# Two hybrid layers, two mixture-of-experts layers: the last experts are taken out of the loop and the overflow section moves ahead of the row selections

## The reference, cut to what matters

```python
def _hier_moe(h, w_group, b_group, w_router, b_router, w_gate, w_up, w_down):
    ...                       # each token: one of 4 groups, then the best 2 of its 8 experts
    def expert_block(args):
        xe, e = args
        return (jax.nn.silu(xe @ w_gate[e]) * (xe @ w_up[e])) @ w_down[e]
    ...                       # y of a token: its two experts' rows, weighted and summed

for i in range(DEPTH):        # DEPTH = 2; 512 tokens, and 256 context tokens in layer 0
    ...
    y = _hier_moe(tokens, ...)
    x = x + gt_f * y[:b * n].reshape(b, n, d)
    if not last:
        xc = xc + gtc_f * y[b * n:].reshape(xc.shape)
return _rmsnorm(x, g_final)
```

## Time and profile before

| | us |
|---|---|
| median of 3 runs | 2984.36 |
| lowest, highest run | 2981.99, 2987.34 |
| time of the profiled execution | 2984.36 |
| its span (first to last instruction) | 2982.4 |
| mean granted TensorE clock | 0.972 of full speed |

### The profile page before, as it was taken

How to read it: one execution, slowest core, us unless ns; L and a number is a source line. 1 busy time by engine, 2 the same in 40 slices (tenths; PEclk the granted TensorE clock), 3 DMA queues, 4 the chain that set the end, 5 groups by cost and what they waited for, 6 DMA issues and landing times. The chain is left out here.

```text
span 2982.4 us, 64978 instructions
## 1 busy us (share of the span) xinstructions
PE 2814.4 (94%) x27057; PEld 1646.5 (55%) x27057; DVE 1143.4 (38%) x2779; ACT 751.1 (25%) x1584; POOL 323.8 (11%) x584
## 2 busy tenths in 40 slices
PE   8999999999989999997999999979999799999996
PEld 4444655444654456645666666634565466666663
DVE  2572753572753345454221112163443611122114
ACT  1111531111542146511111111142664211111111
POOL 3000520000530000011001000120000100000101
PEclk9999999999989999998999999999999899999998
DMA  7212652212743100236999999962002599999993
GB/s 266 72 57 85 234 154 96 85 57 71 245 161 134 57 1 2 109 135 250 400 405 399 398 394 400 352 207 80 2 2 107 210 385 400 399 404 402 400 396 133
DMA packets 155503, 636.93 MB, mean 214 GB/s; under 512 B 19744, under 2 KB 24352, under 8 KB 138960
## 3 DMA queue, kind: packets, MB, share of 16 engines
q1 hardware_dynamic: 114624, 517.59, 44.9%
q0 software_dynamic: 40720, 117.18, 11.6%
HBM read 582.70 MB, written 52.00 MB: 213 GB/s over the span
## 5 line engine op out<-in xcount | busy, mean ns | idle before, releaser
L1052 PE MATMUL PJ<-WR,XT 128*128 128x512 f32 (+2 forms) x1152 | 478.9, 572 | 5.9 <-ACT XT L140 3.3
L140 ACT ACTIVATE PT<-TR 128x512 f32<-128x512 f32 (+3 forms) x384 | 177.8, 493 | 902.8 <-PE TR L1270 735.4
L1052 PEld LDWEIGHTS PJ<-WR,XT 128*128 128x128 f32 x1152 | 217.3, 192 | 246.7 <-issue 219.9
L140 DVE TENSOR_TENSOR PR<-G 128x384 f32<-128x384 f32 x64 | 35.7, 559 | 748.3 <-ACT G L140 747.5
L1020 PE MATMUL PJ<-WR,XT 128*128 128x512 f32 x576 | 259.7, 608 | 2.1 <-ACT XT L140 1.4
L1250 PE MATMUL SC<-QK,XT 128*64 128x256 f32 x2112 | 243.1, 384 | 0.0
L140 DVE TENSOR_REDUCE SM<-SC 128x1 f32<-128x768 f32 (+6 forms) x208 | 173.7, 835 | 168.7 <-PE SC L1093 161.9
L1201 PE MATMUL PJ<-WR,XT 128*128 128x512 f32 x512 | 228.7, 599 | 8.6 <-issue 8.6
L1250 PE MATMUL SC<-WR,XT 128*64 128x256 f32 x1984 | 226.2, 381 | 0.0
L1250 PEld LDWEIGHTS SC<-QK,XT 128*64 128x64 f32 x2112 | 149.7, 138 | 85.7 <-issue 14.9
L1093 PE MATMUL SC<-QK 64*128 64x512 f32 (+7 forms) x512 | 187.7, 528 | 9.4 <-ACT PR L140 9.4
(11 more groups left out here) (243 smaller groups left out, 3346.0 us busy)
## 6 DMA issues: line engine op xcount, KB each, us to landing
QK<-in_w_gate_dram SPq DMA_DIRECT2D x34, 2048.0 KB, 9.3
WR<-in_w_down_dram SPq DMA_DIRECT2D x34, 2048.0 KB, 15.6
QK<-in_w_up_dram SPq DMA_DIRECT2D x32, 2048.0 KB, 14.0
WR<-in_w_up_dram SPq DMA_DIRECT2D x32, 2048.0 KB, 14.1
WR<-in_w_gate_dram SPq DMA_DIRECT2D x30, 2048.0 KB, 9.4
QK<-in_w_down_dram SPq DMA_DIRECT2D x30, 2048.0 KB, 15.8
WR<-in_w_ada_dram SPq DMA_DIRECT2D x24, 2048.0 KB, 7.9
WR<-in_w_in_dram SPq DMA_DIRECT2D x14, 2048.0 KB, 7.7
```

The source lines that it names most:

```text
L140: return lambda *a, **k: Signal(make(*a, **k), self)
L1052: m = mm(bank[:, 0:n], XT1[:, c, s.t * P:(s.t + 1) * P], w[:, c, 0:n], start=c == 0, stop=c == DC - 1)
```

## The change

- **Loop.** PE's and ScalarE's hardware loops run 14 passes, not 15. Step 29 is written out behind it, then `gate_up(31)`, `turn_hidden(30)`, `gate_up_rest(31)`, the turns of the selection matrices, `down(30)`, and the last step without a look ahead (`turn_hidden(31)`, `down(31)`). The 33rd gather and `turn_x` are gone.
- **Selections.** Only `select(s, 0, 0)` stays ahead of the overflow section. `select(s, 0, 1)` and tile 1's two selections go behind it, into the `combine` steps. PE now waits for `pj_free` (the last expert's rows) and for `sc_free` before it loads `count`.
- **VectorE.** `near_sum` of tile 1 moves from `combine` 1 to ahead of the overflow section. In layer 0 its first part (`choices_sum`) stood behind combine 0's last addition; it is now part of `near_sum`.
- **Overflow.** Gate, up and the selection of an overflow block use the free bank of `SC` in place of `PJ`, and the hardware loop over the three blocks of a group is written out three times on every engine. One wait of VectorE's body is gone.
- Semaphore counts follow from that.

The diff, without the lines that only follow from those:

```diff
@@ -487,7 +487,7 @@
...
-        moe = add("moe", l=l, bc=bc, last=last, tiles=moe_tiles, xe0=[16 * 17 * l, 16 * 16 * l], tr=take("tr", 4 + 3 * EXPERTS),
+        moe = add("moe", l=l, bc=bc, last=last, tiles=moe_tiles, xe0=[16 * 16 * l] * 2, tr=take("tr", 4 + 3 * EXPERTS - 2),
@@ -1318,36 +1318,38 @@
...
                     step(once, 0)
-                    with pe.Fori(0, EXPERTS // 2 - 1) as i:
+                    with pe.Fori(0, EXPERTS // 2 - 2) as i:
                         for r in (1, 2):
                             step(lambda a, b: i * a + b, r)
-                    turn_hidden(once, EXPERTS - 1)
+                    step(once, EXPERTS - 3)
+                    gate_up(once, EXPERTS - 1)
+                    turn_hidden(once, EXPERTS - 2)
+                    gate_up_rest(once, EXPERTS - 1)
                     pe.wait_ge(sel_ready, s.l + 1)
                     for g in range(2):
-                        use = s.tr[g - 2]
+                        use = T0 + 3 * EXPERTS - 1 + g
                         pe.wait_ge(tr_free, use - 1)
...
                         x.then_inc(tr_full, 1)
-                    down(once, EXPERTS - 1)
+                    down(once, EXPERTS - 2)
+                    step(once, EXPERTS - 1, ahead=False)
 
...
                     select(s, 0, 0)
+
+                    o = over[s.l]
                     pe.wait_ge(pj_free, s.pj[-1] + 1)
-                    select(s, 0, 1).then_inc(sc_full, 1)
                     pe.wait_ge(sc_free, s.sc[EXPERTS - 1] + 1)
-                    select(s, 1, 0)
-                    select(s, 1, 1).then_inc(sc_full, 1)
-
-                    o, near = over[s.l], s.near
                     pe.wait_ge(over_ready, s.l + 1)
+                    side, near = s.sc[EXPERTS - 1] % 2, s.near
                     count = pe.value_load(OVI[0:1, MAX_OVER:MAX_OVER + 1], min_val=0, max_val=MAX_OVER)
...
                         with pe.If(j < count):
-                            with pe.Fori(0, OVER_GROUP) as b:
+                            for b in range(OVER_GROUP):
                                 pe.wait_ge(o["x"], j * 16 + 16 * b + 16)
@@ -1359,7 +1361,8 @@
...
-                                        x = mm(PJ[:, k, :], XETO[:, c, :], w[:, c, :], start=c == 0, stop=c == DC - 1)
+                                        x = mm(SC[:, side, k * 512:(k + 1) * 512], XETO[:, c, :], w[:, c, :], start=c == 0,
+                                               stop=c == DC - 1)
@@ -1381,15 +1384,20 @@
...
-                                        x = mm(PJ[:, h, :], SLOTTOKO[:, t * P:(t + 1) * P],
+                                        x = mm(SC[:, side, h * 512:(h + 1) * 512], SLOTTOKO[:, t * P:(t + 1) * P],
...
-                elif s.kind == "combine" and s.near and s.t >= 2:
-                    pe.wait_ge(sc_free, s.moe.sc[EXPERTS + s.t - 2] + 1)
-                    select(s.moe, s.t, 0)
-                    select(s.moe, s.t, 1).then_inc(sc_full, 1)
+                elif s.kind == "combine" and s.near:
+                    m, t = s.moe, s.t
+                    if t == 0:
+                        select(m, 0, 1).then_inc(sc_full, 1)
+                    else:
+                        if t >= 2:
+                            pe.wait_ge(sc_free, m.sc[EXPERTS + t - 2] + 1)
+                        select(m, t, 0)
+                        select(m, t, 1).then_inc(sc_full, 1)
@@ -1610,20 +1618,25 @@
...
                     hidden(once, 1)
-                    with act.Fori(0, EXPERTS // 2 - 1) as i:
+                    with act.Fori(0, EXPERTS // 2 - 2) as i:
                         for r in (1, 2):
...
                             hidden(lin, r + 1)
-                    hidden_turned(once, EXPERTS - 1)
+                    hidden_turned(once, EXPERTS - 3)
+                    x_in(once, EXPERTS - 1)
+                    hidden(once, EXPERTS - 2)
+                    hidden_turned(once, EXPERTS - 2)
                     for g in range(2):
-                        use = s.tr[g - 2]
+                        use = T0 + 3 * EXPERTS - 1 + g
                         act.wait_ge(tr_full, use + 1)
                         copy(SLOTTOK[g][0:CAP, 0:s.near * P], TR[0:CAP, use % 2, 0:s.near * P]).then_inc(tr_free, 1)
-
-                    a.count[tr_free.name] += 6 * (EXPERTS // 2 - 2)
-                    a.count[sc_free.name] += 2 * (EXPERTS // 2 - 2) + s.near
+                    hidden(once, EXPERTS - 1)
+                    hidden_turned(once, EXPERTS - 1)
+
+                    a.count[tr_free.name] += 6 * (EXPERTS // 2 - 3)
+                    a.count[sc_free.name] += 2 * (EXPERTS // 2 - 3) + s.near
                     a.latest = (tr_free, a.count[tr_free.name])
@@ -1640,18 +1653,19 @@
...
+                    side = s.sc[EXPERTS - 1] % 2
...
-                            with act.Fori(0, OVER_GROUP) as b:
+                            for b in range(OVER_GROUP):
...
-                                A(GSI[0], PJ[:, 0, :], ACT.Silu)
-                                copy(UPS[0], PJ[:, 1, :]).then_inc(o["act"], 1)
+                                A(GSI[0], SC[:, side, 0:512], ACT.Silu)
+                                copy(UPS[0], SC[:, side, 512:1024]).then_inc(o["act"], 1)
@@ -1741,12 +1755,6 @@
...
-            def choices_sum(f):
-
-                y0, y1 = NEAR_Y[f.t]
-                dve.wait_ge(y_scaled, f.scaled)
-                now(STT(y0, y1, W12[:, 6 + f.t:7 + f.t], y0, ALU.mult, ALU.add))
-
@@ -1761,8 +1769,8 @@
...
                 else:
-                    if f.t == 0:
-                        choices_sum(f)
+                    dve.wait_ge(y_scaled, f.scaled)
+                    now(STT(y0, y1, W12[:, 6 + f.t:7 + f.t], y0, ALU.mult, ALU.add))
                     now(TT(y0, y0, BC[:, 0:D], ALU.mult))
@@ -2032,7 +2040,7 @@
...
-                    if s.t:
+                    if s.t >= 2:
@@ -2045,8 +2053,6 @@
...
-                        if s.t == 0:
-                            choices_sum(s.moe.f[1])
@@ -2349,18 +2355,18 @@
...
-                    dve.wait_ge(xs_loaded[s.f[1].fin % 2], 16 * s.f[1].load)
+                    near_sum(s.f[1])
...
-                    near = s.near
+                    side, near = s.sc[EXPERTS - 1] % 2, s.near
...
-                            with dve.Fori(0, OVER_GROUP) as b:
+                            for b in range(OVER_GROUP):
@@ -2378,14 +2384,13 @@
...
-                                    rows_, x = PJ[:, :, :].rearrange("p a n -> p (a n)"), x_rows_of(f)
+                                    rows_, x = SC[:, side, :], x_rows_of(f)
...
-                                dve.wait_ge(o["added"], j * near + near * b + near + 1)
@@ -2664,7 +2669,6 @@
...
-                    gather(once, EXPERTS, slice(EXPERTS, EXPERTS + 1))
@@ -2681,10 +2685,10 @@
...
-                            with pool.Fori(0, OVER_GROUP) as b:
+                            for b in range(OVER_GROUP):
...
-                                    pool.wait_ge(xe_loaded[k], s.xe0[k] + 16 * (17 - k))
+                                    pool.wait_ge(xe_loaded[k], s.xe0[k] + 16 * 16)
```

More of the change, by code:

```diff
@@ L983, in _ @@
                     with sp.If(j < count):
-                        with sp.Fori(0, OVER_GROUP) as b:
+                        for b in range(OVER_GROUP):
                             e = sp.value_load(OVI[0:1, bass.ds(j + b, 1)], min_val=0, max_val=EXPERTS - 1)
@@ L2629, in _ @@
                     T0, J0 = s.tr[0], s.pj[0]
-                    gathers0 = 33 * s.l
+                    gathers0 = 32 * s.l
                     def gather(at_, r, e):
```

## The result

The changed kernel takes 2999.82 us (median of 5 runs, 2997.36 to 3004.28) against 2984.01 us for the kernel before (5 runs, 2981.99 to 2987.34): a ratio of 1.0060 with an interval of 1.0045 to 1.0075, or **+15.8 us**, slower. The forecast was 2991.0 us, +6.65. The same kernel on another chip later gave 1.0057 (1.0044 to 1.0069), +17 us. Ratios leave out slow executions, of which there was one: 4771.9 us at a mean clock of 0.555, in the second group of run 7.

The account below looks back on a forecast made before the run. PE bounds the expert loop; behind the last `down`, VectorE largely sets the tails. Layer 1 -0.57 + 3.87, layer 0 +1.35, packets +2.0: +6.65 on 2984.36 gives 2991.0 us; own range 2987 to 2995, 8-in-10 2979 to 3000.

Parts of the forecast that it names:

- the sign: Whole kernel: the change makes it slower, +6.65 us; chance of slower 0.48.
- the place: The change acts at the ends of both layers, behind the last `down`, not in the expert loop.
- the loop part: Last expert steps: dropping the 33rd expert and moving selection turns saves 0.7 us in layer 0, 0.57 in layer 1.
- the wait ahead of the count: Overflow section: PE's selections now stand behind the load of `count` and group skip, 4.9 us layer 0, 4.6 layer 1.
- the longer jumps: PE's overflow `If` jumps over three written-out bodies; first jump fetches one packet, +1.0 us a layer, bounds 0 to 2.
- 8 more matmuls of 0.43 us: Layer 1 tail: tile 1's addition needs these on PE after tile 0's addition, +3.43 us, to 2957.7.
- the 2.09 us from selection to addition: Layer 1 tail: time from `select(0,1)` on PE to VectorE's addition of tile 0, taken over from the earlier trace.
- rival 4: Overflow sections: every long jump of PE fetches, +13 to +25 us, so 3004 to 3016; chance 0.12.
- The second: `gate_up_rest(31)`: starvation goes as the code leaves the loop, 6.95 us layer 1, 4.6 layer 0, 2979.4; chance 0.12.
- The first: Both tails: VectorE's moved work is worth more and the skip costs less, balancing at about 2986; chance 0.1.
- third: Overflow section: `count` loads earlier and the new order hides the skip, 3 us a layer back; chance 0.06.

Follow-up runs that it names:

- run 7: Kernel before with the loop part, `near_sum(1)` ahead of the overflow section, short loops, and an If on count > 0 on all engines: ratios 0.9984 and 0.9980.
- run 9: Kernel before plus nine test skips behind PE's last work, with 84 transfers of 2 MB beside them; first long jumps waited 6.0 to 6.7 us.
- run 11: Changed kernel with PE's short hardware loop over overflow blocks and five unread matmuls ahead of the load of `count`: ratio 0.9999, -0.3 us on the kernel before.
- the changed kernel's second run: The changed kernel, unaltered, run and traced again on another chip: ratio 1.0057 to the kernel before, +17 us.
- run 1: Changed kernel with PE's three overflow blocks back in a short hardware loop, other engines' bodies still written out: ratio 1.0018, +5.4 us on the kernel before.
- run 5: Changed kernel with 32 tiny matmuls at PE's start, shifting its later code by half a fetched block: ratio 1.0056, +16.7 us on the kernel before.
- the ladder: Nine test loops with failing Ifs, added to the kernel before behind PE's last work; idle transfers: first jumps two or more blocks on waited 3.3 to 3.7 us.
- the second traces: The kernel before and the changed kernel, each unaltered, traced again on another chip: ratio 1.0057, +17 us.
- run 8: Kernel before with the ladder and no transfers beside it; no whole-kernel ratio given, later jumps took 0.22 us.
- run 4: Kernel before with only the changed selection order, moved `near_sum` and `SC` bank; 15 passes and short loops: ratio 1.0019, +5.6 us.
- run 12: Changed kernel with short hardware loops and an If on count > 0 around the group loop on all five engines: ratio 0.9991, -2.7 us on the kernel before.

## Why the prediction was wrong in its size

**Right: the sign, the place, the loop part.** PE's skip, moved ahead of the selections, is what sets both tails. The loop part measured -0.8 and -0.6 us without starvation (forecast -0.7 and -0.57). Beside that, layer 0's starvation was shorter in the changed kernel (stage a -3.4 and -5.0 us in the two pairs), which no term had. Run 9, whose expert loops are those of the kernel before, takes 22.0 there, against 24.5 and 26.2 in that kernel's own traces: so that stage varies without the change, and how much of the gain is the change's stays open.

**Right within 1 us: the wait ahead of the count, at full clock.** Run 11 against the kernel before: layer 0 +2.0 us (forecast, without the loop part, +2.05), layer 1 +3.0 (forecast +3.87; the skip took 3.7 us, not 4.5).

**The step that failed: the longer jumps.** The mechanism was as written, a first jump a layer to code that isn't held. The term was "one packet: +1.0 us a layer", with two packets as the upper bound. It measured, as the changed kernel's second run less run 1, 35.6 - 28.5 = 7.1 us in layer 0 and 51.1 - 47.3 = 3.8 in layer 1: 11 us for 2 (run 5 less run 1: 6.0 and 3.6). The bound was wrong because it took a packet's own time, 0.9 us, for the wait. A wait of 3.7 us in the ladder holds 1.0 us until the packet starts, 1.3 for it, and 1.4 more; and beside transfers, as in layer 0, the packet starts only 4.2 to 5.3 us behind the branch. ("Nothing in the trace jumps as far" holds for jumps ahead: the expert loop's own jump back passes 1004 instructions, which are kept.)

**A smaller step that failed: the clock.** "8 more matmuls of 0.43 us" and the 2.09 us from selection to addition held the clock at 1.00. Run 1 less run 11 gives what it costs: 28.5 - 26.7 = 1.8 us in layer 0 and 47.3 - 45.1 = 2.2 in layer 1. The earlier trace rows were read as the price of a selection, when they were its price directly behind other matmuls.

**The sum.** Layer 0: 2.0 + 1.8 + 7.1 = 10.9, the whole of stage b. Layer 1: 3.0 + 2.2 + 3.8 = 9.0, stage c (51.1 - 42.1). These must add up, as each term is the difference of two rows of the table. The check is the whole time. Less stage a, 5.0 and 0.8, they give +14.1 us between the second traces, against +17 (13.1 to 20.6) by the runs. Without starvation, run 5's stages less those of run 8, with 42.1 for its stage c, give -0.8 + 9.8 - 0.6 + 8.8 = +17.2, against +16.7 by the runs. The 8-in-10 range ended at 3000 and just holds the 2999.8, but it was drawn that wide for rival 4, not for a wait of this length; the forecast's own range, 2987 to 2995, doesn't hold it.

**The rivals.** The fourth, every long jump fetches, came closest with its 3004 to 3016, but by luck: it added 14 jumps at 0.9 to 1.8 us each, and what came was one wait a layer, of 3.8 to 7.6. The second, no starvation out of the loop, is false: both traces of the changed kernel starve. The first and third are false by stages b and c.

## What to carry to other kernels

A section that is nearly always passed over should be left by one short jump, or stand where queued work covers it: the same waits, 10 us in all, cost nothing behind queued selections and 11 us ahead of them. Before unrolling a body, count the blocks of 256 instructions between branch and target; price a miss by a whole fetch with the DMA load of that moment, not by the packet. And where an edit opens a gap on PE, price the matmuls behind it at the lower clock.

## What the runs showed of the hardware

- A first jump to code two or more blocks on held PE's sequencer for 3.3 to 4.0 us with idle DMA engines (ladder, and layer 1 of the kernels) and 6.0 to 6.7 with busy ones (run 9); 6.2 to 7.6 in layer 0, where weights were arriving. Repeats took 0.22 us at any length up to five blocks.
- A jump into the very next block waited 3.8 us too (3.1 in run 9) when the branch stood 8 instructions into its own.
- PE's granted clock was 0.50 behind gaps of 4.6 us (run 1, layer 0) and of 3.8 us (run 1, layer 1), and 1.00 behind ones of 0.4 us (run 11) and 1.0 to 1.1 us (run 12). Behind one of 3.6 us (run 4, layer 1) it was 1.00 for 1.3 us more and then 0.50.
- PE starved for about 7 us under POOL's gathers in layer 1 in every trace of two groups of runs, and in none of the other three; the medians of the kernel before differ by 9 to 13 us with it. The cause is not known.
